# Two units side by side in the block loops behind two double norms, and two more in the score banks

## The reference, cut to what matters

```python
x = x + rmsnorm(cross_out, norm_cross_post)      # post norm of the cross attention
h = rmsnorm(x, norm_ffn_pre)                     # pre norm of the feed-forward part
gate, up = split(h @ w_ffn_in)                   # 2 x 2816 columns
gate = causal_dwconv(gate, conv_w) + conv_b      # width 3
x = x + rmsnorm((silu(gate) * up) @ w_ffn_out, norm_ffn_post)
h = rmsnorm(x, attn_norm_e_2)                    # pre norm of the even mixer
qa, ka, va, qb, kb, vb = split(h @ w_in_e)       # 18 blocks of 128 columns
```

## Time and profile before

| | |
|---|---|
| median of 3 runs | 2260.61 us (2259.1 to 2261.63) |
| the profiled execution: its time / its span | 2259.95 / 2258.2 us |
| PE busy | 2167.3 us (96%), 10034 matmuls |
| DVE / ACT / POOL busy | 47% / 38% / 36% |
| mean granted clock of PE | 0.984 |
| one POOL subtraction (L487), one ACT raise (L1208) | 2418 ns, 1059 ns |
| block loop of `fup0`, of `even_in` | about 444 to 461 us, 823 to 841 us |

### The profile page before, as it was taken

The page is one execution under the profiler, slowest core; times in us unless marked ns, Lnnn a source line. Parts: engine busy times, 40 slices in busy tenths (PEclk is TensorE's granted clock), DMA queues, the critical chain, the costliest instruction groups (busy, mean ns, idle before and its releaser), DMA issues.

```text
span 2258.2 us, 27123 instructions
## 1 busy us (share of the span) xinstructions
PE 2167.3 (96%) x10034; PEld 1721.1 (76%) x10034; DVE 1055.5 (47%) x1530; ACT 853.8 (38%) x1276; POOL 819.3 (36%) x343
## 2 busy tenths in 40 slices
PE   7899899899999988997999999999999999999999
PEld 5775588778888865764888888888888877888887
DVE  5765646585525263357532312336753766322121
ACT  6435544432222242445442322334432444423231
POOL 3321235144444432210444444443333324444443
PEclk9899999999999999999999999999999999999999
DMA  4222123123322331110233232232222212323223
GB/s 152 66 66 70 62 75 103 47 84 116 112 98 93 107 126 56 61 43 1 94 96 100 93 101 95 96 101 72 75 84 84 76 47 87 100 93 100 96 94 102
DMA packets 54967, 193.36 MB, mean 86 GB/s; under 512 B 6096, under 2 KB 6352, under 8 KB 54480
## 3 DMA queue, kind: packets, MB, share of 16 engines
q1 hardware_dynamic: 50400, 181.58, 24.6%
q10 hardware_dynamic: 4464, 10.36, 1.4%
HBM read 189.82 MB, written 2.10 MB: 85 GB/s over the span
## 4 chain that ended last, share of the span: by engine, by line
PE 87%; DVE 9%; ACT 2%; issue 1%; DMA 1%; SPq 0%; DVEq 0%; ACTq 0%
PE gemm_ps L518 25%; PE gemm_ps L519 25%; PE gemm_ps L520 25%; PE out_ps L962 2%; DVE xl L1753 1%; PE score_ps L954 1%; DVE x L1780 1%; PE turn_ps L749 1%; DVE arena L1753 1%; PE out_ps L759 1%; PE score_ps L928 1%; PE score_ps L740 1%; DVE tmp L1753 1%; DVE y_all L1899 1%; DVE y_all L1916 0%
## 5 line engine op out<-in xcount | busy, mean ns | idle before, releaser
L487 POOL TENSOR_TENSOR wl<-raw,wh 128x1024 fp32r<-128x1024 f32 x339 | 819.1, 2418 | 1420.7 <-ACT wh L1208 1420.7
L1208 ACT ACTIVATE wh<-raw 128x1024 fp32r<-128x1024 f32 x339 | 358.9, 1059 | 754.0 <-DMA raw<-w_in 737.3
L518 PE MATMUL gemm_ps<-xh,wh 128*128 128x512 f32 x1512 | 610.1, 404 | 32.1 <-DVE xl L1753 16.5
L519 PE MATMUL gemm_ps<-xl,wh 128*128 128x512 f32 x1512 | 592.2, 392 | 0.0
L520 PE MATMUL gemm_ps<-xh,wl 128*128 128x512 f32 x1512 | 591.9, 391 | 0.0
L519 PE MATMUL gemm_ps<-arena_r,wh 128*128 128x512 f32 (+1 forms) x1088 | 417.2, 383 | 0.0
L518 PEld LDWEIGHTS gemm_ps<-xh,wh 128*128 128x128 f32 x1512 | 286.0, 189 | 111.0 <-issue 32.1
L519 PEld LDWEIGHTS gemm_ps<-xl,wh 128*128 128x128 f32 x1512 | 286.3, 189 | 64.1 <-issue 6.9
L520 PEld LDWEIGHTS gemm_ps<-xh,wl 128*128 128x128 f32 x1512 | 286.0, 189 | 60.7
L518 PE MATMUL gemm_ps<-arena_r,wh 128*128 128x512 f32 (+1 forms) x832 | 320.0, 385 | 2.9 <-DVE x L1849 2.9
L520 PE MATMUL gemm_ps<-arena_r,wl 128*128 128x512 f32 (+1 forms) x832 | 317.6, 382 | 0.0
(11 more groups left out here) (367 smaller groups left out, 2078.8 us busy)
## 6 DMA issues: line engine op xcount, KB each, us to landing
raw<-w_in SPq DMA_DIRECT2D x339, 512.0 KB, 3.3
arena<-na_in ACTq DMA_DIRECT2D x14, 256.0 KB, 2.7
x<-x_in SPq DMA_DIRECT2D x8, 256.0 KB, 6.6
out<-x ACTq DMA_DIRECT2D x8, 256.0 KB, 2.7
arena<-alibi_in ACTq DMA_DIRECT2D x6, 256.0 KB, 3.4
con<-con_in SPq DMA_DIRECT2D x1, 1432.0 KB, 11.8
arena<-moba_in ACTq DMA_DIRECT2D x1, 1024.0 KB, 4.9
arena<-mem_in ACTq DMA_DIRECT2D x1, 1024.0 KB, 4.9
```

The lines of the kernel that those rows point to most:

```text
L487: pool.tensor_tensor(wl[:, k, :], raw[:, k, :], wh[:, k, :].bitcast(F32), ALU.subtract).then_inc(unit_split, 1)
L518: pe.matmul(o, wh[:, n % RING, w], h[:, kt, 0:width], start=(kt == 0), stop=False)
L519: pe.matmul(o, wh[:, n % RING, w], l[:, kt, 0:width], start=False, stop=False)
L1208: act.activation(wh[:, k % RING, :], raw[:, k % RING, :], ACT.Copy).then_inc(high_split, 1)
```

## The change

Behind both double norms the first two units go through the blocks together: for each block PE makes three products of each unit, into both banks of `gemm_ps`, and then the column sum; for the last block the column sum goes ahead of the products. The next two units are made into the two banks of `score_ps`. Units 5 and 6 use `gemm_ps` again and wait for `emptied` at n-3, that is for the unit four before. From unit 7 on (`fup0` only) the old rule holds. DVE drains the first four from where they lie. Since the second unit's predecessor isn't finished early any more, and four units are wanted soon, ACT raises the fourth unit (`n0 + 3`) ahead of the first block; before, that raise stood behind the root. Cut to its core:

```diff
+        def early_bank(n0, n):
+            return score_ps[:, n - n0 - 2, :] if n - n0 in (2, 3) else gemm_ps[:, n % 2, :]
...
+            def early_units(n0, h, l):
+                pe.wait_ge(unit_split, n0 + 2)
+                pe.wait_ge(emptied, n0)
+                for kt in range(KT):
+                    pe.wait_ge(rhs_ready, blocks_split[0] + kt + 1)
+                    if kt == KT - 1:
+                        column_sum(kt)
+                    for n in (n0, n0 + 1):
+                        piece(n, early_bank(n0, n), kt, kt + 1, h, l)
+                    if kt < KT - 1:
+                        column_sum(kt)
+                blocks_split[0] += KT
+                for n in (n0 + 2, n0 + 3):
+                    pe.wait_ge(unit_split, n + 1)
+                    piece(n, early_bank(n0, n), 0, KT, h, l)
+
+            def next_unit(n, h, l):
+                pe.wait_ge(unit_split, n + 1)
+                pe.wait_ge(emptied, n - 3)
+                piece(n, gemm_ps[:, n % 2, :], 0, KT, h, l)
...
             token_norm(apart=2)
-            units(FIRST["fup0"], 1, xh, xl, fresh=True, summing=True)
-            units(FIRST["fup0"] + 1, 2 * FF1_PARTS[0] - 1, xh, xl)
+            fup0 = FIRST["fup0"]
+            early_units(fup0, xh, xl)
+            for n in (fup0 + 4, fup0 + 5):
+                next_unit(n, xh, xl)
+            units(fup0 + 6, 2 * FF1_PARTS[0] - 6, xh, xl)
...
             token_norm()
-            units(FIRST["even_in"], 6, xh, xl, fresh=True, summing=True)
+            early_units(FIRST["even_in"], xh, xl)
+            for u in (4, 5):
+                next_unit(FIRST["even_in"] + u, xh, xl)
...
-            prepare(x, "norm_ffn_pre", xh, lambda b: take(block_ready))
+            def split_after(n):
+                def ready(b):
+                    if b == 0:
+                        raise_to(n + 3)
+                    take(block_ready)
+                return ready
+            prepare(x, "norm_ffn_pre", xh, split_after(FIRST["fup0"]))
...
             def split_and_loaded(b):
+                if b == 0:
+                    raise_to(FIRST["even_in"] + 3)
                 take(block_ready)
```

More of the change, by code:

```diff
@@ L1782, in add_normed, with scaled @@
                     low(x, pre, xh, xl, b - 1)
-            def scaled(n, dst, s=None, rows=P, width=N, rs=None, factor=1.0, src=None, bank=None):
+            def scaled(n, dst, s=None, rows=P, width=N, rs=None, factor=1.0, src=None, bank=None, ps=None):
                 dve.wait_ge(unit_done, n + 1)
-                a = gemm_ps[0:rows, n % 2 if bank is None else bank, 0:width]
+                a = gemm_ps[0:rows, n % 2 if bank is None else bank, 0:width] if ps is None else ps
                 r = (rstd if rs is None else rs)[0:rows, 0:width]
@@ L2181, in gated @@
                         n, t, u = FIRST[f"fup{p}"] + 2 * i, tmp[:, b % 2, :], padded[b % 2]
-                        scaled(n, u[:, 2:N + 2])
+                        scaled(n, u[:, 2:N + 2], ps=early_bank(FIRST["fup0"], n))
                         convolve(t, u, [p_("ffn_conv_w", 22 * k + b) for k in range(3)], conv_ready)
@@ L2185, in gated @@
                         dve.wait_ge(unit_done, n + 2)
-                        done(dve.tensor_tensor(t, sq[:, b % 2, :], gemm_ps[:, (n + 1) % 2, :], ALU.mult), emptied)
+                        done(dve.tensor_tensor(t, sq[:, b % 2, :], early_bank(FIRST["fup0"], n + 1), ALU.mult), emptied)
                         done(dve.tensor_tensor(t, t, rstd[:, :], ALU.mult))
@@ L2296, in _ @@
             for b in range(6):
-                scaled(FIRST["even_in"] + b, proj2[:, b, :])
+                scaled(FIRST["even_in"] + b, proj2[:, b, :], ps=early_bank(FIRST["even_in"], FIRST["even_in"] + b))
             done(dve.memset(eps[:, 2:3], 0.0), proj_raw)
```

## The result

The changed kernel takes 2268.46 us (median of 7 runs, 2266.88 to 2271.57), beside 2260.84 (7 runs, 2258.94 to 2265.27) for the kernel before on the same chip: 1.0032 times as long, interval [1.0021, 1.0043]. The profiled execution takes 2267.33, its span grew from 2258.2 to 2265.5. The forecast was 2264.5 and its range ended at 2267.5: the loss came, by the mechanism forecast, and 3 to 4 us larger. The profiled execution still lies inside the range, by 0.2, and the median 1.0 outside it.

A forecast was written before the change was run, and what follows sets the result against it. The prediction took PE to bound the kernel, with 87% of the span. A loss of 6.2 us at `fup0` less a gain of 1.7 at `even_in` gave +4.5 on 2259.95, so 2264.5 us; range 2257.5 to 2267.5.

The forecast's parts named there:

- the subtraction on the first add: Before the block loop, POOL's early subtraction delays DVE's `x` adds: 1.8 us at `fup0`, 1.0 at `even_in`.
- the PE-bound loop: In the block loop a block costs PE 2.24 us, just under DVE's 2.30, so a late start is never made up.
- the later first drain: Behind the norm before `fup0`, DVE's first drain comes at 468.4, 2.9 us later than before.
- PE idle before unit 59: In `fup0`, PE stands 5.6 us waiting for unit 57's drain and starts unit 59 4.6 later than before.
- a small gain at `even_in`: At `even_in` the first two units are out earlier, gaining 1.7 us, ends 0 and 2.7.
- The chain from the first drain to that of unit 57: DVE's work in `fup0` between these drains: 13.2 us bare plus 11 of POOL's hits.
- Rival A: Mild stall at unit 59: POOL hits as little as before, idle 2 us, clock kept; 2259.4 us, chance 0.27.
- rival B: Faster: POOL misses the norms' adds and unit 57 is drained by 487; 2254.4 us, chance 0.13.
- Rival C: Worse: the block loop gets into ACT, blocks stretch by up to 0.5 us each; with the stall 2268, chance 0.10.
- the term for the half clock: PE runs at half clock after idling: full about 3.4 us after the first block, some 3.3 us behind the stall.
- The start of the loop: At `fup0`, block 0's products take 2.67 us at half clock; 19.5 from first product until both units are out.
- The clock behind the stall: After the idle before unit 59, PE runs some 3.3 us at half clock, adding 1.6 us.

The follow-up runs named there:

- e4: Changed kernel, with the units of `fup0` and `fup1` going around four banks instead of two; 2262.45 us, 1.0008 of the kernel before.
- e8: Changed kernel, but POOL subtracts only half the low weights of units 57 to 61, ACT copies the rest; 2263.18 us, 1.0008 of the kernel before.
- e5: e4 with the raise of the fourth unit put back behind the root; 2260.03 us, 0.9993 of the kernel before.
- e3: Changed kernel with the raise of the fourth unit put back behind the root; 2265.3 us, 1.0009 of the kernel before.
- e10: Kernel before, with only the raise of the fourth unit moved ahead of block 0 in both norms; 2264.77 us, 1.0008 of the kernel before.
- e6: e5 plus eight products that nothing reads ahead of block 0 in both norms; 2254.97 us, 0.9972 of the kernel before.
- e11: Kernel before, with only eight products that nothing reads ahead of the block loop in both norms; 2263.23 us, 0.9999 of the kernel before.

## Why the prediction was right and wrong

**Right: where it would go.** All that was named ahead is there: the subtraction on the first add, the PE-bound loop, the later first drain, POOL working twice in a row and each hit nearly whole, PE idle before unit 59, half a clock behind it, a small gain at `even_in`. The chain from the first drain to that of unit 57 was put at 24.2 (13.2 bare and 11 of POOL) and measured 23.5. e4 and e8 each take one link out, the two banks and POOL's hits; each ends the stall, and F falls by 8.2 and 8.7. Rival A fell with the 5.26 of idle, rival B with the gap and the long add. Rival C came out by number only (2268), which is luck: squares and `xl` do wait for column sums, by 1.01 and 1.41 at the end of the loop, but that shows DVE and ACT following PE; at full clock the blocks on PE stay 2.25 apart, so nothing stretched them.

**Wrong: the sizes, nearly all by the clock.** The step that failed is the term for the half clock: the sum took it to last 3.4, 3.3 and 2.9 us in the loop of `fup0`, behind the stall and in `even_in`, and it lasted 5.8, 6.1 and 4.7.

- *The start of the loop.* The prediction has "products of block 0 take 0.57 + 5 x 0.42 = 2.67 at half clock", and from block 1 on the sum used full speed, because the earlier trace rows showed the clock full 3.4 us behind the first product. It was full 5.8 us behind it. First product to the end of column sum 7 took 19.6 instead of 18.3 (the sum's own terms give 18.1). Ahead of it the spread ran at half clock (2.08 for 1.16, +0.9), which lies ahead of the changed code, and the add was held 1.14 instead of 1.8. Together the first drain comes 1.7 later than the sum had it (471.12 - 1.05 against 468.4), and less 0.7 for the shorter chain that makes unit 59 start 5.6 later, not 4.6.
- *The clock behind the stall.* "I add 1.6 for some 3.3 us at half clock": it was about 6.1 us and 2.8.
- *`even_in`.* Gain 1.09 for 1.7. The add was held 0.98, as forecast (1.0); the clock was full 4.7 us behind the first product (833.91 to 838.6) and not 2.9.

8.4 - 1.1 is +7.3 for the +4.5 forecast: 1.0 more before unit 59, 1.2 behind the stall, 0.6 at `even_in`. The 1.0 holds the 0.9 of the late spread, which I count as bad luck: with the spread in time the profiled execution would have taken some 2266.4 (an estimate, 2267.33 less 0.92). The common failure is that one measured time to full clock was taken as a property of the chip. Over the profiles it came 2.9 to 6.1 us behind the first real product where nothing ran ahead of it. The old loop never told its price, because PE had spare time in it; the new one has none. The range should have carried that time as a bound of its own at all three places; with twice the length at each, by the prediction's own price of 1.6 for 3.3 us, it would have reached past 2268 (an estimate).

**Not settled.** What decides how long the half clock lasts, and when it falls. At `fup0` it lasted longer where more time lay between the fall and the first product: 3.4 us in the kernel before (6.8 in all), 4.4 to 5.3 in e8 and e4 and 6.5 to 7.3 in e5 and e3 (all four 10.2), 7.8 in the changed kernel and e10 (13.6). So a part of the loss that I put down to the clock, 2.0 in e3's comparison, hangs on the moment of the fall as well as on the raise. Only one execution of each kernel was profiled; how often the others had the late spread isn't known.

## What to carry to other kernels

A head start behind a norm is worth only as much as the engine that drains it can follow: before giving PE a lead, walk the drainer's chain to the first bank that is used again, with POOL's subtractions at full hits, and give the lead as many banks as the lateness needs. An early raise has its price even where the engine that does it is idle: it moves a POOL subtraction onto whatever DVE does then. And once a loop is bound by PE, its clock at the start counts in full, so idle time ahead of it can be filled with products that nothing reads. In these runs they gained 1.5 and 1.3 us (e6) and cost nothing where they didn't help (e11).

## What was not expected of the hardware

- PE being busy did not end the half clock soon: in the changed kernel it worked without a pause from 447.07 to 452.9 before the clock rose, in e6 at `even_in` the half clock was over after 3.4 us in all. From e11, timeline of PE and stretches:

```profile
441.93 2.09 PE L567 MATMUL out_ps<-wh 128*128 128x512 f32 x8
446.12 0.50 PE L518 MATMUL gemm_ps<-xh,wh 128*128 128x512 f32 x1 [2.10 <-DVE xl L1757]
...
443.00:445.00 2.00, 1.02 (x5) 0.51 (x3) 1.90 (x4) 1.20 (x2) 0.00 (x0) 1.00 0.00 0
...
447.00:449.00 2.00, 2.00 (x4) 0.82 (x4) 1.93 (x3) 0.72 (x1) 0.00 (x0) 0.50 0.00 0
```

  Behind eight products at full clock it stayed full through the next 2.1 us of idling, and fell at 446.6, while real work was already running; with nothing there it had fallen in the idle time.
- Two subtractions queued on POOL let one DVE instruction through between them: beside the changed kernel's pair of 5.27 a CAST (2.51) and a TENSOR_TENSOR (2.77) were each held once and each finished beside one half of the pair. So DVE got 1.1 us of work done (0.43 + 0.69) in 5.3.
